# Feed-forward up product of a transformer block with the weights as the stationary operand

## The reference

```python
u2 = rmsnorm(h, g_mlp_pre[i])
ff = jnp.square(jax.nn.relu(u2 @ w_up[i])) @ w_down[i]
h = h + rmsnorm(ff, g_mlp_post[i])
```

## Time and profile before

| What | Value |
|---|---|
| Median of 3 executions | 2624.75 us (2621.5 to 2626.97) |
| Profiled execution, its own time | 2625.25 us |
| Its span, first to last instruction | 2623.5 us |
| Mean granted TensorE clock | 0.998 of full |
| Instructions | 30290 |

### The profile page before, as it was taken

How to read it: one execution, slowest core, us unless ns; L and a number is a source line. 1 busy time by engine, 2 the same in 40 slices (tenths; PEclk the granted TensorE clock), 3 DMA queues, 4 the chain that set the end, 5 groups by cost and what they waited for, 6 DMA issues and landing times.

```text
span 2623.5 us, 30290 instructions
## 1 busy us (share of the span) xinstructions
PE 2593.4 (99%) x11884; PEld 2141.0 (82%) x11884; DVE 1706.9 (65%) x1827; ACT 1229.9 (47%) x1620; POOL 38.3 (1%) x84
## 2 busy tenths in 40 slices
PE   8999999999999999999999899999999999999998
PEld 7888888888888888888888788888888888788887
DVE  5656555556766666666676667767777787445655
ACT  5444444444744444444446643443443445544544
POOL 0000000000000000000000100000000000000000
PEclk9999999999999999999999999999999999999999
DMA  7554465556677777777766567777777777454343
GB/s 264 176 175 163 171 210 193 192 186 225 225 273 257 264 265 255 263 266 249 265 224 224 177 199 265 267 260 259 272 260 257 274 277 219 142 192 153 104 144 129
DMA packets 277461, 579.36 MB, mean 221 GB/s; under 512 B 16480, under 2 KB 56032, under 8 KB 264160
## 3 DMA queue, kind: packets, MB, share of 16 engines
q1 hardware_dynamic: 255376, 466.65, 53.5%
q10 hardware_dynamic: 21968, 111.09, 11.4%
HBM read 575.58 MB, written 2.11 MB: 220 GB/s over the span
## 4 chain that ended last, share of the span: by engine, by line
PE 96%; DVE 1%; ACT 1%; DMA 0%; issue 0%; POOL 0%; SPq 0%; DVEq 0%; POOLq 0%; ACTq 0%
PE panels L564 26%; PE panels L565 26%; PE panels L569 26%; PE spare L643 3%; PE spare L565 2%; PE spare L564 2%; PE spare L569 2%; PE spare L684 2%; PE panels L583 1%; PE panels L589 1%; PE panels L584 1%; DMA raw<-w_in 0%; ACT work L1173 0%; PE spare L908 0%; PE spare L918 0%
## 5 line engine op out<-in xcount | busy, mean ns | idle before, releaser
L1791 DVE TENSOR_TENSOR lo<-raw,hi 128x1024 fp32r<-128x1024 f32 x830 | 1004.8, 1218 | 701.2 <-ACT hi L1135 699.6
L1135 ACT ACTIVATE hi<-raw 128x1024 fp32r<-128x1024 f32 x830 | 871.7, 1056 | 1129.3 <-PE panels L569 1002.0
L564 PE MATMUL panels<-hi,xT_hi 128*128 128x512 f32 x1960 | 771.9, 394 | 7.0 <-ACT hi L1135 7.0
L565 PE MATMUL panels<-hi,xT_lo 128*128 128x512 f32 x1960 | 764.3, 390 | 0.0
L569 PE MATMUL panels<-lo,xT_hi 128*128 128x512 f32 x1960 | 525.3, 390 | 0.0
L564 PEld LDWEIGHTS panels<-hi,xT_hi 128*128 128x128 f32 x1960 | 368.7, 188 | 82.3 <-DVE xT_lo L1971 6.9
L569 PEld LDWEIGHTS panels<-lo,xT_hi 128*128 128x128 f32 x1960 | 368.5, 188 | 77.3
L565 PEld LDWEIGHTS panels<-hi,xT_lo 128*128 128x128 f32 x1960 | 368.8, 188 | 74.8
L564 PE MATMUL panels<-hi,yT_hi 128*128 128x512 f32 (+1 forms) x988 | 385.9, 391 | 1.3 <-ACT acc L1706 1.3
L565 PE MATMUL panels<-hi,yT_lo 128*128 128x512 f32 (+1 forms) x988 | 381.4, 386 | 0.0
L569 PE MATMUL panels<-lo,yT_hi 128*128 128x512 f32 (+1 forms) x988 | 261.0, 386 | 0.0
(11 more groups left out here) (292 smaller groups left out, 1862.3 us busy)
## 6 DMA issues: line engine op xcount, KB each, us to landing
work<-k_ada_w ACTq DMA_DIRECT2D x96, 1024.0 KB, 6.7
raw<-w_in SPq DMA_DIRECT2D x79, 1024.0 KB
raw<-w_up SPq DMA_DIRECT2D x64, 1024.0 KB
raw<-w_down SPq DMA_DIRECT2D x64, 1024.0 KB
raw<-ret_w_in SPq DMA_DIRECT2D x64, 1024.0 KB
raw<-ret_w_in SPq DMA_DIRECT2D x64, 512.0 KB
raw<-ret_w_out SPq DMA_DIRECT2D x32, 1024.0 KB
raw<-mla_w_in SPq DMA_DIRECT2D x24, 1024.0 KB
```

The costliest lines, as they stand in the source:

```text
L564: pe.matmul(o, x_hi[:, kt0 + j, ms], hi_at(k)[:, at], start=first and j == 0, stop=False)
L565: pe.matmul(o, x_lo[:, kt0 + j, ms], hi_at(k)[:, at], start=False, stop=False)
L1135: act.activation(hi_at(k)[:, 0:words], raw[:, slot, k % 2 * CHUNK:k % 2 * CHUNK + words], copy).then_inc(hi_ready, 1)
L1791: dve.tensor_tensor(lo_at(k)[:, 0:words], raw[:, k // 2 % RAW_SLOTS, k % 2 * CHUNK:k % 2 * CHUNK + words], hi_at(k)[:, 0:words].bitcast(F3 ...
```

## The change

Up panels 1 to 15 are made by `weights_chunk` in place of `chunk`. A 128 x 128 piece of the weights is stationary; the columns that move are tokens. For a piece of `hi`, 512 columns move: 256 of x_hi and 256 of x_lo, which now lie in one tile `xT`. For a piece of `lo`, 256 columns of x_hi move. That makes 8 + 8 products per chunk. A panel is four banks (512 hidden columns as 4 x 128 partitions, 256 + 256 columns): `panels` for even and `spare` for odd panels. The result is already transposed, so PE makes no transposes for these panels. ACT copies the first halves to `up`, DVE adds the second halves, ACT applies Relu, squares, and copies to `yT_hi`, DVE subtracts to `yT_lo` (`up_step`, steps 0 to 4 in successive chunks). The scale 1/rms is left out of the up panels; since relu and square are homogeneous, its square (`st_up2`) multiplies at the end: ACT's squares take it as their scale, and POOL multiplies the last 1/rms by it. The down product uses four panels in turn and one semaphore `ffn_taken` in place of `panel_taken`. The first up panel is made and transposed as before, without the scale, and transposed into `panel[1]`.

The diff, cut to its core and moved left:

```diff
+UPS = FF // N
+FFN_ORDER = [("up", u) for u in range(1, 4)]
+for block in range(FF // FF_BLOCK):
+    FFN_ORDER += [("down", 4 * block + n) for n in range(4)] + [("up", u) for u in (2 * block + 4, 2 * block + 5) if u < UPS]
+def ffn_banks(kind, i):
+    return range(i % 2 * 4, i % 2 * 4 + 4) if kind == "up" else range(i % 4 * 2, i % 4 * 2 + 2)
+def ffn_count(kind, i):
+    return FFN_ORDER.index((kind, i)) + 1
+def ffn_count_of_banks(kind, i):
+    banks = set(ffn_banks(kind, i))
+    return max((n + 1 for n, p in enumerate(FFN_ORDER[:ffn_count(kind, i) - 1]) if banks & set(ffn_banks(*p))), default=0)
...
-xT_hi, xT_lo = sb("xT_hi", [P, KT, TOKENS], F32R), sb("xT_lo", [P, KT, TOKENS], F32R)
+xT = sb("xT", [P, 2, KT, TOKENS], F32R)
+xT_hi, xT_lo = xT[:, 0], xT[:, 1]
...
-panel = [panels[:, 0:TILES, :], panels[:, TILES:2 * TILES, :], spare[:, 0:TILES, :]]
+panel = [panels[:, 0:TILES, :], panels[:, TILES:2 * TILES, :], spare[:, 0:TILES, :], spare[:, TILES:2 * TILES, :]]
...
+up = carve(8192, 4, TOKENS)
+st_up2 = stats[:, 84:86]
...
+    def weights_chunk(banks, s):
+        k = t.count(lo_ready)
+        parts = [(j, g, slice(j * N + g * P, j * N + (g + 1) * P)) for j in range(2) for g in range(4)]
+        def hi_products():
+            for j, g, at in parts:
+                done = pe.matmul(banks[:, g, :].rearrange("p (c t) -> p c t", c=2), hi_at(k)[:, at], xT[:, :, 2 * s + j, :],
+                                 start=s == 0 and j == 0, stop=s == 7 and j == 1)
+            return done
+        def lo_products():
+            pe.wait_ge(lo_ready, t.nth(lo_ready))
+            for j, g, at in parts:
+                done = pe.matmul(banks[:, g, 0:TOKENS], lo_at(k)[:, at], xT_hi[:, 2 * s + j, :], start=False, stop=False)
+            return done
+        pe.wait_ge(hi_ready, t.nth(hi_ready))
+        if s < 7:
+            hi_products()
+            done = lo_products()
+        else:
+            lo_products()
+            done = hi_products()
+        done.then_inc(multiplied, 1)
+        t.nth(multiplied)
...
-    def up_turns(b):
-        panel_closed(b)
+    def first_up_turns():
+        panel_closed(0)
+        panel_closed(1)
         for j in range(2):
-            turn_tokens(j, lambda m: relu[:, m, j * 2 * P:(j + 1) * 2 * P])
-    def down_chunk(s, k):
-        wide_chunk(s % 4, s // 4 % 2, YT[k], 4)
-    for s in range(8, 32):
-        if s in (10, 18, 26):
-            up_turns(s // 8 % 2 ^ 1)
-        wide_chunk(s % 8, s // 8 % 2, XT)
-    for i in range(3):
-        for s in range(64):
-            if s in (2, 34):
-                up_turns(1)
-            if s in (26, 58):
-                up_turns(0)
-            if s % 32 < 16:
-                down_chunk(s, s // 32)
+            turn_tokens(j, lambda m: relu[:, m, j * 2 * P:(j + 1) * 2 * P], panel[1][:, j, :])
+    def up_chunk(u, s):
+        banks = spare if u % 2 else panels
+        if s == 0:
+            if u == 1:
+                for b in range(2):
+                    turn_closed(b)
+                    score_closed(b)
+            elif u == 2:
+                for b in range(2):
+                    panel_closed(b)
+                    turn_closed(b)
             else:
-                wide_chunk(s % 8, s // 8 % 2, XT)
-    for s in range(32):
-        if s == 2:
-            up_turns(1)
-        down_chunk(s, s // 16)
+                pe.wait_ge(ffn_taken, ffn_count_of_banks("up", u))
+        weights_chunk(banks, s)
+    def down_chunk(block, s):
+        n = s // 4
+        if s % 4 == 0:
+            pe.wait_ge(ffn_taken, ffn_count_of_banks("down", 4 * block + n))
+        chunk(n, YT[block % 2], 2 * (s % 4), s % 4 == 0, s % 4 == 3)
+    for u in range(1, 4):
+        for s in range(8):
+            if u == 1 and s == 2:
+                first_up_turns()
+            up_chunk(u, s)
+    for block in range(8):
+        for s in range(16):
+            down_chunk(block, s)
+        for u in (2 * block + 4, 2 * block + 5):
+            for s in range(8 if u < UPS else 0):
+                up_chunk(u, s)
     for s in range(8):
+        if s in (0, 2):
+            pe.wait_ge(ffn_taken, ffn_count("down", FF // FF_BLOCK * 4 - 4 + s // 2))
+        if s == 6:
+            pe.wait_ge(ffn_taken, len(FFN_ORDER))
         if s >= 6:
             turn_h(s - 6)
         if s % 2 == 0:
...
-    def up_panel(b):
+    def first_up_panel():
         chunks_done()
-        each_tile(relu, b, ACT.Relu).then_inc(act_step, 1)
+        for m in range(TILES):
+            done = act.activation(relu[:, m, :], panel[0][:, m, :], ACT.Relu)
+        done.then_inc(act_step, 1)
         act.wait_ge(act_step, t.nth(act_step))
-        act.activation(relu, relu, ACT.Square).then_inc(panel_taken[b], 1)
-        t.nth(panel_taken[b])
-    def up_hi(b, k):
+        act.activation(relu, relu, ACT.Square).then_inc(panel_taken[0], 1)
+        t.nth(panel_taken[0])
+    def first_up_hi():
         for j in range(2):
-            hi_plain(j, yT_hi[k], slice(b * 4 + 2 * j, b * 4 + 2 * j + 2))
-    def by_dve(s):
-        if s in (4, 8, 12, 16):
-            t.nth(panel_taken[s // 4 % 2 ^ 1])
+            wait_turned(j)
+            act.activation(yT_hi[0][:, 2 * j:2 * j + 2, :], two(panel[1][:, j, :]), copy).then_inc(turn_hi, 1)
+    def up_step(u, step):
+        if step == 0:
+            chunks_done()
+            act.activation(up, (spare if u % 2 else panels)[:, :, 0:TOKENS], copy).then_inc(up_half, 1)
+            t.nth(up_half)
+        if step == 2:
+            act.wait_ge(ffn_taken, ffn_count("up", u))
+            act.activation(up, up, ACT.Relu).then_inc(act_step, 1)
+            act.wait_ge(act_step, t.nth(act_step))
+            act.activation(up, up, ACT.Square).then_inc(act_step, 1)
+        if step == 3:
+            act.wait_ge(act_step, t.nth(act_step))
+            half = slice(u % 2 * 4, u % 2 * 4 + 4)
+            act.activation(yT_hi[u // 2 % 2][:, half, :], up, copy).then_inc(turn_hi, 1)
+    def ff_squares(n):
+        act.wait_ge(ffn_taken, ffn_count("down", 28 + n))
+        for m in range(TILES):
+            done = act.activation(relu[:, m, :], acc[:, m, n * N:(n + 1) * N], ACT.Square, scale=st_up2[:, m:m + 1],
+                                  accum_out=st_parts[:, m, n:n + 1])
+        done.then_inc(squares_done, 1)
...
+    for block in range(7):
+        for s in range(32):
+            ada_loads(s, ada_at(32), 0, lambda n: slice(((block + 1) * ADA_PER_32 + n) * P, ((block + 1) * ADA_PER_32 + n + 1) * P))
+            if s < 4:
+                up_step(2 * block + 3, s)
+            if s >= 24 and block < 6:
+                up_step(2 * block + 4, s - 24)
+            if s in (20, 24, 28) and block == 6:
+                if s == 20:
+                    wait_rstd()
+                ff_squares(s // 4 - 5)
...
+    def first_up_lo():
+        for j in range(2):
+            turned_hi()
+            dve.tensor_tensor(yT_lo[0][:, 2 * j:2 * j + 2, :], two(panel[1][:, j, :]), yT_hi[0][:, 2 * j:2 * j + 2, :].bitcast(F32),
+                              ALU.subtract).then_inc(turn_taken[j], 1)
+    def up_step(u, step):
+        if step == 1:
+            dve.wait_ge(up_half, t.nth(up_half))
+            dve.tensor_tensor(up, (spare if u % 2 else panels)[:, :, TOKENS:N], up, ALU.add).then_inc(ffn_taken, 1)
+            assert t.nth(ffn_taken) == ffn_count("up", u)
+        if step == 4:
+            turned_hi()
+            half = slice(u % 2 * 4, u % 2 * 4 + 4)
+            dve.tensor_tensor(yT_lo[u // 2 % 2][:, half, :], up, yT_hi[u // 2 % 2][:, half, :].bitcast(F32), ALU.subtract)
+    def down_panel(block, s):
         if s in (4, 8, 12, 16):
             n = s // 4 - 1
             chunks_done()
             part = acc[:, :, n * N:(n + 1) * N]
-            dve.tensor_tensor(part, panel[n % 2], part, ALU.add).then_inc(panel_taken[n % 2], 1)
-            t.nth(panel_taken[n % 2])
+            dve.tensor_tensor(part, panel[n], part, ALU.add).then_inc(ffn_taken, 1)
+            assert t.nth(ffn_taken) == ffn_count("down", 4 * block + n)
...
-    def rstd_of_sum(width):
+    def rstd_of_sum(width, product=None):
         pool.tensor_scalar(st_rstd, st_sum, 1.0 / width, EPS, ALU.mult, ALU.add).then_inc(pool_step, 1)
         pool.wait_ge(pool_step, t.nth(pool_step))
-        pool.tensor_tensor(st_rstd, st_rstd, neg_half[:, 0:TILES], ALU.pow).then_inc(rstd_ready, 1)
+        done = pool.tensor_tensor(st_rstd, st_rstd, neg_half[:, 0:TILES], ALU.pow)
+        if product is not None:
+            done.then_inc(pool_step, 1)
+            pool.wait_ge(pool_step, t.nth(pool_step))
+            done = pool.tensor_tensor(product[0], st_rstd, product[1], ALU.mult)
+        done.then_inc(rstd_ready, 1)
...
-    for _ in range(3):
-        rstd_parts()
+    rstd_parts((st_up2, st_rstd))
+    rstd_parts((st_rstd, st_up2))
+    rstd_parts()
```

(67 more changed lines are left out.)

31 lines of the change are left out of this document (2 added, 29 removed).

## The result

| | before | after |
|---|---|---|
| Median of 20 executions each | 2624.75 us (2621.5 to 2627.26) | 2620.04 us (2616.72 to 2622.52) |
| Profiled execution, its own time (span) | 2625.25 (2623.5) | 2618.43 (2616.6) |
| Instructions | 30290 | 31005 |

The ratio is 0.9984, interval 0.9978 to 0.9990: faster by 4.7 us (0.18%), where 13.3 were forecast. First the window of the feed-forward stage in both kernels, here from the first product behind the first up panel to the last down addition (columns as in the earlier trace rows; before, then after), then the transposes and the two new DVE steps of the changed kernel by line (697 is `turn_batch`, 2323 the addition, 2329 the subtraction).

What follows compares the result with a forecast made beforehand. PE's own stream was taken to bound the feed-forward stage. Terms -13.6 + 0 + 0 + 0.3 = -13.3 us gave 2612.0 us for the profiled execution and a median of 2611.5, with an 8-in-10 range of 2608.5 to 2620.

Steps and rivals of the forecast that it cites:

- 8 x 226.7 + 8 x 113.3 = 2720 ns: 0 us: In up-panel chunks, eight hi and eight lo products take PE as long as the old twelve products: 0 us.
- a few ns of hand-over: Possible extra time at each lo product's weight load; 4 ns would be +3.8 us.
- Transposes: In the feed-forward stage, 15 groups of eight transposes leave PE's stream at 0.905 us each: -13.6 us.
- No gain in the stream: In up-panel chunks, a gain below 0 us from the new products is excluded, as the moving columns' pace is unchanged.
- ACT and DVE: Over 15 up panels ACT works 11 and DVE 16 us more, beside 372 and 224 us idle: 0 us.
- PE's new waits: PE's waits for ffn_taken name banks closed at least eight chunks earlier, so they are free: 0 us.
- The end: At the stage's end POOL gets one more two-element product on the path: +0.3 us, bounds 0.2 to 1.3.
- The load-share rule: By busy share of weight loads, 83%, the stage would become load-bound: +34.6 us; the prediction refused it as a price.
- The rival by that rule: Load-bound chunks in the stage, +34.6 - 13.3: 2646 us; given within the unhidden-load case, whose chance was 0.06.
- Rival (a): Weight loads pace lo products at 117 to 127 ns, not 113.3: 2615 to 2624 us, middle 2620; chance 0.12.
- sign of a load that costs something: Chunks of 2.76 us or more in the up product, where 2.72 was forecast, would show the prediction wrong.

Runs made afterwards that it cites:

- Experiment 2: The changed kernel with the lo products of up panels 1 to 15 made with 64 columns of weights in place of 128: 2614.18 us.
- experiment 1: The changed kernel with hi products of chunks 1 to 6 of up panels 1 to 15 made with 64 columns of weights in place of 128: 2617.9 us.
- Experiment 3: The changed kernel with 320, then all 512 columns moving in the lo products of up panels 1 to 15 in place of 256: 2644.91 and 2718.91 us.
- experiment 5: The kernel before, with each lo product of up panels 1 to 15 cut into two of 256 columns, each with its own full load: 2634.66 us.
- experiment 6: The kernel before, with six of the eight transposes left out for each of up panels 1 to 15: 2615.76 us, ratio 0.9964.

## Why the prediction was wrong

**The step that failed** is "8 x 226.7 + 8 x 113.3 = 2720 ns: 0 us". It took 2793. It has two parts.

First, the lo products: 113 ns once and then 119 to 120, not 113.3, which is 953 against 907 ns a chunk, 46 to 47 more, and 5.6 us in all. The argument was that 0.11 us from load to load fits into 0.113. But those loads stood behind transposes, not under an fp32r product with 256 moving columns, and the pace of the earlier trace rows is one with a 64-column load. In the earlier trace rows eight loads share 1.31 us, 0.164 each; only the sharing out by columns made 0.11 of it. So no row had a full load every 0.113 us in a steady stream. I gave "a few ns of hand-over" a price (4 ns, 3.8 us) and then left it out of the sum. Experiment 2 shows that the difference goes with the width of the load; the stage gets 5.0 of the 5.6 us back.

Second, the hi products behind the short ones: some 27 ns in every chunk but a panel's first, 24 ns in the mean of all, 2.9 us in all. No rival had this. It was visible, though, in the trace before. Behind the short MLA products the next eight of 512 columns take 1.84 us, not 1.81 (chain; 992 is a short product, 564 and 565 the long ones, 569 the first of the next group):

```profile
2273.88 0.11 PE panels L992
2273.99 0.23 PE panels L564
2274.22 0.23 PE panels L565
...
2275.83 0.23 PE panels L569
```

2273.99 to 2275.83 is 1.84 us. I read the pace inside the group of short products and not what followed it. The same effect hid in the 0.905 us of the earlier trace rows, which I read as one difference of starts:

```profile
1006.54 0.87 PE spare L643 x8
1007.42 0.23 PE panels L564
```

The eight transposes take 0.87 us, and the eight long products behind them 1.84, from 1007.42 to the 1009.26 of the earlier trace rows. Experiment 2 shows that the effect does not hang on the width of the short products' loads; with narrow loads under the long products (experiment 1) it is 19 ns in place of 27. Experiment 3 shows that it goes when no product is short, and experiment 5 that it is no matter of layout. What in the chip makes it stays open, as does why a full load under 256 columns takes 120 ns.

Point by point for the rest. **Transposes**, -13.6: right. 15 groups are gone, and experiment 6, which took out transposes alone, gained what they were reckoned at. **No gain in the stream**: right. **ACT and DVE**, +11 and +16 us beside idle time: they grew by 11.3 and 14.9 us in the windows above, and no product of the stage waited for them. **PE's new waits**: none appeared in the stage; 8 us behind it PE waited once for a lo split, 0.5 us (yT_lo, line 595), beside a chain that ran over DVE. **The end**, +0.3: the chain from the last addition to the transposes of h was 1390.81 - 1378.33 = 12.48 us and is

```profile
1371.49 1.24 DVE acc L2337
...
1377.32 0.21 POOL stats L2786
...
1384.43 0.63 PE spare L697 x4
```

1384.43 - 1371.49 = 12.94: +0.46. Of this POOL's steps up to DVE's start are 0.28 (3.29 us in place of 3.01), as forecast, with the new product from 1377.32 on; the other 0.18 lie ahead of POOL (2.85 in place of 2.67 us from the addition's start), in the step of ACT's squares.

**The load-share rule** of the Trainium skill ("Trainium Kernel Development and Optimization", Best Practices) judges how near TensorE is to its limit by the busy share of its weight loads, with a second measure beside it. The rival by that rule, 2646, did not come, and the rule was rightly refused as a price: 16 load records of 187 to 192 ns stand in a chunk of 2.79 us, over 100% of it, and over the stage the records add up to 96% where they were 84%, while the time fell. (The busy share of the profile, which counts overlapping records once, is 584.49 / 684.14 = 85%.) As a warning it had a point, since full loads under short products did cost something.

```profile
L633 PEld LDWEIGHTS spare<-xT,lo x512: 187/192/192, 688.9 to 1282.2; 128*128 128x128 f32 x171
```

**Rival (a)**, the lo products paced by their loads at 117 to 127 ns, is the first part of what happened: 120 ns. That the 2620.04 us are its middle is partly luck: the lo products alone give 2611.5 + 5.6 = 2617.1, and the 2.9 us of the slow hi products, which no rival had, make it 2620.0. I held it unlikely, because I took a pace from products with other loads for the pace of the columns, and the range ended at 2620.0, at that rival's middle. The prediction's own sign of a load that costs something, chunks of 2.76 us or more, did come: 2.79. The change is a gain, but one of 0.18% and not of over 0.2%.

## What to carry to other kernels

A product's pace in a trace belongs to its whole shape: columns moved, columns loaded, and what stood before it. When a change makes long products into short ones, look for the same pair of load and moving width, and read also the products that follow a run of short ones; if the trace has no such pair, leave room for it in the range: here 960 short products cost 6 ns each, 5.6 us, and the long ones behind them 2.9 us more. A saving that is exactly counted (15 groups of transposes at 0.905 us) can be right and still be two thirds spent by a stream that looked equal in columns.

## What the runs showed of the hardware

In fp32r with 128-column loads, 512 moving columns take 226.7 ns in a steady stream (1.81 us for eight, with no short product near), and in groups of eight behind long products 320 columns take some 146 and 256 columns 119 to 120. With 64-column loads 256 take 113.3, and 113 to 117 in experiment 2. After a run of eight products of 256 columns, with loads of 128 or of 64 columns, five products of 512 columns with full loads take 228 to 236 ns. Strictly alternating 512 and 256 columns have two steady paces, 347 and 353 ns a pair (2773 and some 2827 a chunk), and one extra long product at the right place moves the stream from the slow one to the fast one.
